# Moving the streamed operand Y from directly behind the split weights to a place next to X

## The reference, cut to what matters

```python
def first_block(x, ...):
    proj = rmsnorm(x, norm_mix_g) @ w_in          # 1024 x 9232
    y_a = short_conv_branch(bg, cg, xv, conv_a_w) @ w_a_out
    y_b = gdn_branch(q, k, v, z, a, b, ...) @ w_b_out
    x = x + (sigmoid(ga) * y_a + sigmoid(gb) * y_b) @ w_o
    h = rmsnorm(x, norm_ffn_g)
    x = x + (silu(gate) * val) @ w_down           # gate, val = split(causal_dwconv(h @ w_up))
    return rmsnorm(x, norm_final_g)

def second_block(x, ...):
    qa, ka, va, qr, kr, vr, gr, gate_a, gate_b = split(rmsnorm(x) @ w_in_2)
    y = sigmoid(gate_a) * (attention(qa, ka, va) @ w_proj_a_2) \
        + sigmoid(gate_b) * (retention(qr, kr, vr, gr) @ w_proj_b_2)
    x = x + y @ w_out_2
    return x + square(relu(rmsnorm(x) @ w_up_2)) @ w_down_2
```

## Time and profile before

| | |
|---|---|
| median of three runs | 1227.18 us |
| span of the profiled execution | 1228.6 us |
| PE busy | 1181.1 us, 9690 matmul instructions |
| DVE, ACT, POOL busy | 779.9, 609.0, 303.7 us |
| mean granted clock of PE | 0.986 |
| a weights block from issue to landing (median) | 4.8 us |

### The profile page before, as it was taken

How to read it: one execution, slowest core, us unless ns; L and a number is a source line. 1 busy time by engine, 2 the same in 40 slices (tenths; PEclk the granted TensorE clock), 3 DMA queues, 4 the chain that set the end, 5 groups by cost and what they waited for, 6 DMA issues and landing times.

```text
span 1228.6 us, 22170 instructions
## 1 busy us (share of the span) xinstructions
PE 1181.1 (96%) x9690; PEld 1154.8 (94%) x9690; DVE 779.9 (63%) x847; ACT 609.0 (50%) x700; POOL 303.7 (25%) x175
## 2 busy tenths in 40 slices
PE   5988999999999799999989999999999999999998
PEld 5887999999999799999979999999999999999998
DVE  5997785545355667677648966655565655755453
ACT  4877432242374365555456543442498444543431
POOL 3343374411022234144235510000011010411010
PEclk9988999999999999999989999999999999999999
DMA  6433332123345444544535444333542554454552
GB/s 239 168 122 136 118 136 70 69 73 140 114 156 206 148 161 172 206 173 171 191 119 202 172 172 172 138 138 139 188 154 104 206 205 173 156 216 179 206 176 100
DMA packets 27744, 192.91 MB, mean 157 GB/s; under 512 B 3072, under 2 KB 3072, under 8 KB 4992
## 3 DMA queue, kind: packets, MB, share of 16 engines
q1 hardware_dynamic: 27648, 191.49, 43.6%
HBM read 190.43 MB, written 1.05 MB: 156 GB/s over the span
## 4 chain that ended last, share of the span: by engine, by line
PE 59%; issue 13%; ACT 10%; DVE 8%; POOL 8%; DMA 2%; POOLq 0%; SPq 0%; ACTq 0%; DVEq 0%
PE psS L527 32%; PE psA L527 9%; PE psS L515 7%; POOL t L1548 6%; ACT wh L847 4%; DVE wl L1164 3%; DVE acc L1167 2%; DMA raw<-in_wts 2%; PE psA L659 1%; PE psA L673 1%; DVE Xl L1167 1%; PE psA L677 1%; ACT L831 1%; POOL ss L1548 1%; DVE gdn L1164 1%
## 5 line engine op out<-in xcount | busy, mean ns | idle before, releaser
L1164 DVE TENSOR_TENSOR wl<-raw,wh 128x2048 fp32r<-128x2048 f32 (+1 forms) x174 | 403.7, 2320 | 212.4 <-ACT wh L847 211.8
L847 ACT ACTIVATE wh<-raw 128x2048 fp32r<-128x2048 f32 x176 | 336.4, 1912 | 305.3 <-PE psS L527 150.9
L527 PE MATMUL psS<-Yh,wh 128*128 128x256 f32 x1056 | 309.2, 293 | 11.6 <-DVE Yl L1167 8.3
L527 PE MATMUL psS<-Yl,wh 128*128 128x256 f32 x1056 | 300.7, 285 | 0.0
L527 PE MATMUL psS<-Yh,wl 128*128 128x256 f32 x1056 | 300.6, 285 | 0.0
L527 PE MATMUL psS<-Xh,wh 128*128 128x256 f32 x896 | 264.6, 295 | 20.4 <-DVE wl L1164 14.1
L527 PE MATMUL psS<-Xl,wh 128*128 128x256 f32 x896 | 251.7, 281 | 0.0
L527 PE MATMUL psS<-Xh,wl 128*128 128x256 f32 x896 | 251.6, 281 | 0.0
L527 PEld LDWEIGHTS psS<-Yh,wh 128*128 128x128 f32 x1056 | 204.5, 194 | 16.9 <-DVE Yl L1167 9.3
L527 PEld LDWEIGHTS psS<-Yl,wh 128*128 128x128 f32 x1056 | 204.7, 194 | 2.5 <-issue 1.9
L527 PEld LDWEIGHTS psS<-Yh,wl 128*128 128x128 f32 x1056 | 204.4, 194 | 0.0
(11 more groups left out here) (239 smaller groups left out, 2146.1 us busy)
## 6 DMA issues: line engine op xcount, KB each, us to landing
raw<-in_wts SPq DMA_DIRECT2D x176, 1024.0 KB, 4.8
xT<-in_x SPq DMA_DIRECT2D x2, 512.0 KB, 6.3
raw<-in_wts SPq DMA_DIRECT2D x2, 512.0 KB, 7.1
gdn<-in_x SPq DMA_DIRECT2D x1, 1024.0 KB, 6.9
out<-xT SPq DMA_DIRECT2D x4, 256.0 KB, 2.2
xT<-in_sel SPq DMA_DIRECT2D x1, 512.0 KB, 6.2
xf<-in_dr SPq DMA_DIRECT2D x1, 512.0 KB, 5.7
xT<-in_mask SPq DMA_DIRECT2D x1, 384.0 KB, 5.5
```

The costliest lines, as they stand in the source:

```text
L527: mm = pe.matmul(bank[:, half], a[:, n % 3, p, :], b[:, kk_, :], start=(first and i == 0), stop=(last and i == 2), skip_group_check=True)
L847: act.activation(wh[:, n % 3], raw[:, n % 2], ACT.Copy).then_inc(sem["wh"], 1)
L1164: dve.tensor_tensor(out, a, b, op).then_inc(sem[name], 1)
```

## The change

The line that allocates `Yh` and `Yl` stands behind `rtok` instead of before `xT`. Nothing else is changed. The order of the instructions is the same on all five engines, as are their waits and shapes; only addresses of Y, xT and the small tiles differ.

```diff
         wh = sb("wh", [P, 3, 16, P], F32R)
         wl = sb("wl", [P, 3, 16, P], F32R)
-        Yh, Yl = sb("Yh", [P, KT, S], F32R), sb("Yl", [P, KT, S], F32R)
         xT = sb("xT", [P, KT, S])
         par = sb("par", [P, NPAR])
         rb, rfin, lnt = sb("rb", [P, S]), sb("rfin", [P, S]), sb("lnt", [P, S])
...
         ss = [sb(f"ss{i}", [P, 2, S]) for i in range(2)]
         small = sb("small", [P, 64])
         rtok = sb("rtok", [P, 2])
+        Yh, Yl = sb("Yh", [P, KT, S], F32R), sb("Yl", [P, KT, S], F32R)
 
 
         with ExitStack() as own:
             Xh, Xl = sb("Xh", [P, KT, S], F32R, own), sb("Xl", [P, KT, S], F32R, own)
         xf = sb("xf", [P, 4096])
```

## The result

The changed kernel took 1217.68 us in the median of four runs (1215.98 to 1219.70), the kernel before 1225.79 us in four runs beside them (1224.39 to 1227.36). The two medians are 8.1 us apart. The ratio on record is 0.9922, or 9.6 us, with a 95% interval of 0.9900 to 0.9944, in which the ratio of the medians (0.9934) lies too: 8 to 10 us faster, where 13 were forecast, and 1217.68 lies in the forecast range of 1208 to 1223. The profiled execution of the changed kernel took 1218.03 us; its span is 1216.1 us.

What follows compares the result with a forecast made beforehand. It took PE as the bound, through the distance between matmul starts. Gains summed to 16.7 us, 12.6 (say 13) after the slow rhythm's losses; subtracted from the median 1227.2 this gave 1214 us, range 1208 to 1223.

Steps and rivals of the forecast that it cites:

- upper bound of 6.7 ns a matmul: Most a Y matmul could gain, from 120 to 113.3 ns between starts; 0.32 us for a block of 48.
- w2 and d2: 12 Y blocks, no wait after, d2 ending the program: 3.7 us gained.
- the slow rhythm: X's second pace, 118 ns between starts instead of 113; Y and X blocks falling into it reduce the 16.7 us sum.
- the place doesn't matter: Rival: Y's address has no effect, the change does nothing, time 1227.2 us; chance 0.14.
- the rival of the border: Rival: a memory border at 131072 cuts Yl and leaves Yh slow; gain at most 5.6 us, 1221.6 us; chance 0.10.
- u1: 22 blocks bound by a 6.36 us round without PE; of 7 us only a last block gains, 0.3 us.
- the slower rival: Rival: longer PE idling in u1 drops the clock to half; six such blocks give about 1237 us; chance 0.06.
- wb: 4 blocks, 1.3 us, ending in PE's wait for `wl`: gain 0.
- qa 3 to gr 3: 35 blocks where PE is never idle: 0.28 us a block, 9.8 us.
- gr 4 to tb 3: 12 blocks where ScalarE takes over soon; half of 3.2 us kept, 1.6 us.
- 40% of the 35 blocks: Share of qa 3 to gr 3 put in the slow rhythm at 118 ns: 3.0 us lost.
- 20% of the 25 blocks of d1, pa, pb and w2: Share of these blocks put in the slow rhythm, X's reset being gone: 1.1 us lost.

Runs made afterwards that it cites:

- e1: Kernel before with Y left directly behind the weights but 64 bytes further, all behind it moved by 128 bytes; 1227.82 us, ratio to before 0.9992.
- e2: Changed kernel with Y 64 bytes further, at a multiple of 128 like the weights; 1235.43 us, ratio to the kernel before 1.0048.
- e3: Kernel before with X, Z and O moved up by 64 bytes to multiples of 128, Y unmoved; 1239.57 us, ratio to before 1.0093.
- f3: Changed kernel with `wl` moved by 64 bytes and all behind it by 256; ratio to the kernel before 1.0049.
- after_again: The changed kernel once more, unaltered, beside new runs of the kernel before; 1218.99 us, ratio to before 0.9921; its profiled execution took 1225.13 us.
- after_third: The changed kernel once more, unaltered, on another chip; 1221.22 us, ratio to the kernel before 0.9938.
- g1: Changed kernel, but in u1 and wb Y lies 320 bytes further, at distance 0 (mod 512) from the weights; 1218.33 us, ratio to before 0.9933.
- g2: Changed kernel, but Y keeps its distance of 192 only in u1 and wb, and is at 0 elsewhere; 1228.69 us, ratio to before 0.9995.

## Why the prediction was right, and where its terms were off

**The cause.** Right: Y is slow for its low address bits (e1, e2, e3), and the weights' bits count too (f3). That it is the two reads that collide, as the prediction put it, fits f3 but no run shows it. The upper bound of 6.7 ns a matmul is what w2 and d2 gained, 3.8 us for a forecast of 3.7. The gain fell short of the 13 us by 3 to 5, nearly all of it on one side: the slow rhythm, which the change lets in, cost more than was put down for it. The range held since its upper end had every block in that rhythm. The rival "the place doesn't matter" fell with the result, the rival of the border with e2. The rule of the Trainium skill ("SBUF — State Buffer", section "Who interferes with whom"), by which TensorE's two read ports are independent and it never waits on anyone, does not describe this stream: 288, 283 and 272 cycles for the same instructions with operands 64 bytes elsewhere.

**u1: right.** ScalarE's `e` follows `e` by 6.36 us as in the earlier trace rows, and PE idles 0.46 us before a block instead of 0.36. Blocks at 113 ns would have made it longer by 0.3, but these run at 118:

```profile
467.35 0.42 ACT L938 ACTIVATE e<-acc 128x256 f32<-128x256 f32 x1
...
473.71 0.42 ACT L938 ACTIVATE e<-acc 128x256 f32<-128x256 f32 x1
```

```profile
474.38 0.36 PE L527 MATMUL psS<-Yh,wh 128*128 128x256 f32 x1 [0.46 <-issue]
```

In one thing the prediction read too much into the earlier trace rows: PE does not idle before every block. In the kernel before it idles before 7 of them, the last of each stage (u1 6 to 9 and 19 to 21), and runs ahead of the round before that. A shorter block makes it catch up sooner: in the changed kernel it idles before 9 blocks, in `after_again` before 12, in all 4.6 and 6.2 us for 2.5 before, while `e` still follows `e` every 6.35 us. So the gain ends as idle time.

The blocks beside u1 0 gave 0.7 us, for a forecast of 0.3. Half clock in the u1 rounds, the slower rival's mechanism, did not come: the page's clock is at nine tenths or more in every slice from the fifth on.

**wb: right, and what looks like a gain is not one.** wb 1 to 3 became 0.11 us shorter each, and wo 0 and 1, now at 118 ns, took it back ahead of the wait for `wl`, which is 0.53 us where it was 0.61. In `after_again` and `after_third`, where wb is at 113, wb 1 to 3 gained 0.96 us and wo 0 and 1 gave 1.0 back, with waits for `wl` of 0.31 us at the start of wo 1 and 1.04 at the start of wo 2: what the prediction said of them. The 0.8 us of the table lie in wb 0: near its end the kernel before waits for the low part of Y,

```profile
377.61 0.38 PE L527 MATMUL psS<-Yh,wh 128*128 128x256 f32 x1 [0.51 <-DVE Yl L1164]
```

and the changed kernel does not, as it comes there 0.9 us later relative to the blocks before: the slow rhythm of gb and z had used up that wait. In g1, with Y in wb at 120 ns and gb and z slow, wb 0 is as short (5.76 us for 5.69, 6.50 before); in g2, with Y freed and gb and z as before, it takes 6.50. What the slow rhythm costs is not lost where a wait follows.

**wa** gave 0.7 us for 1.2 (1.0 in the other two profiles): two of its four blocks were at 118.

**qa 3 to gr 3: the mechanism right, its slow share too small.** PE is the bound, as the earlier trace rows said. The stretch that answers to it has 294 matmuls for 286:

```profile
715.00:749.00 34.00, 34.00 (x294) 34.00 (x293) 19.00 (x17) 11.50 (x6) 0.00 (x0) 1.00 0.50 184
```

I had 9.8 us less 3.0 for 40% of the blocks in the slow rhythm. Measured were 5.0. Of the 35 blocks 17 run at 117 or 118 in the mean, 13 between 114 and 117, where the state changes within the block, and 5 at 113.

**gr 4 to tb 3: right in mechanism, 0.9 us for 1.6.** Each block from gr 4 to ta 3 gained 0.16 us, and tb 0 gave 0.84 back, in the wait for the group norm of the retention branch. Before and after:

```profile
945.89 0.66 PE L811 MATMUL psA<-par,acc 128*128 128x128 f32 x4 [0.32 <-DVE acc L1488]
```

```profile
937.25 0.66 PE L811 MATMUL psA<-par,acc 128*128 128x128 f32 x4 [1.33 <-DVE acc L1488]
```

DVE's `acc` stands behind its `wl`, and that waits for ScalarE's `wh`, in the changed kernel:

```profile
932.66 2.29 DVE L1164 TENSOR_TENSOR wl<-raw,wh 128x2048 fp32r<-128x2048 f32 x1 [3.65 <-ACT wh L847]
...
936.38 0.81 DVE L1488 TENSOR_SCALAR acc<-psA,bag,rsd 128x512 f32<-128x512 f32 x1 [0.60 <-ACT rsd L1109]
```

ScalarE's copies `wh` start at 930.74 and 940.12 us, 9.38 apart; in the kernel before they start at 939.38 and 948.75, 9.37 apart. From the copy at 897.99 us (before) to the one at 948.75, each starts 8.64 or 8.65 us earlier in the changed kernel, while PE's blocks moved from 8.5 us earlier at gr 5 to 9.6 at tb 0 and were back at 8.8 at tb 1. So ScalarE's row of steps is the round of this stretch and was late next, as said; half was too much to hope for.

**u2 0: wrong.** The prediction had "no wait after" w2, but half of w2's 1.26 us was lost here: u2 0 gave 0.65 us back, in a longer wait for the low part of X. Before and after:

```profile
1048.40 0.39 PE L527 MATMUL psS<-Xh,wh 128*128 128x256 f32 x1 [1.09 <-DVE Xl L1167]
```

```profile
1038.53 0.39 PE L527 MATMUL psS<-Xh,wh 128*128 128x256 f32 x1 [1.75 <-DVE Xl L1167]
```

**The terms that were mis-sized most** are those of the slow rhythm. The first, "40% of the 35 blocks", took 4.8 us and not 3.0. The second is "20% of the 25 blocks of d1, pa, pb and w2 (1.1 us lost)". It said rightly that X would lose its reset, but it took each block as a draw by itself, and whole stretches go one way: all 11 blocks of d1 went slow (+2.3 us), while pa to d2 stayed fast. In `after_again` d1 stayed fast and pa to d2 went slow. And gb and z were put at nothing: they lost the same 0.91 us in all three profiles of the changed kernel, so this part is set by the program.

From the 12.6 us forecast to the 7.9 measured outside the norms: qa 3 to gr 3 takes 1.8, gr 4 to tb 3 0.7, the slow rhythm 2.3 (d1 1.2 more than forecast, gb, z and the blocks before 1.1), u2 0 0.65 and wa 0.5; wb, u1 and w2 return 1.3.

## What to carry to other kernels

When the same matmul form has two durations by operand, look at the addresses of both operands modulo 256 first; here 64 bytes of padding decide on 6% of the pace. Sweep that distance on the chip, with the whole stream in view: the padded kernel e1 cured its slow operand and gained nothing, since the same padding shifted all tensors behind it. And judge by stretches of fixed length with the count of matmuls in them, in more than one profile, since one kernel has several rhythms.

## What the runs showed of the hardware that I had not expected

- Back-to-back matmuls of 256 float32r columns with a new 128x128 stationary tile each have mean paces that go with the distance of the two operands modulo 256: 288 cycles at 0 and 96, 280 at 32, 284 to 286 at 128, 281 to 286 at 160, 280 to 285 at 224, and either 272 or 283 at 64 and 192.
- At 64 and 192 the pace has two stable states of one program. A state lasts for up to tens of blocks; pauses and matmuls of another kind can end it. It differs between profiles: 71, 86 and 62 slow blocks in three profiles of one kernel. The stretch from pa to the end alone is worth some 9 us, 0.75%.
- With one matmul in three at another distance (f3) none of the 177 blocks kept the 272 cycles.

What stays open is why 64 and 192 differ, what in the engine makes the pace hang on the addresses, and what sets the state at the start of a stretch.
